# A transformer block's feed-forward: transposes of sixteen pieces, and transposes by quadrant with an exchange through HBM

## The reference

```python
h2 = rms_norm(x, norm_ffn_g[l])
u = jnp.square(jax.nn.relu(jnp.einsum('bsd,df->bsf', h2, w_up[l])))    # 2048 -> 8192
x = x + jnp.einsum('bsf,fd->bsd', u, w_down[l])                        # 8192 -> 2048
return rms_norm(x, norm_final_g)
```

## Time and profile before

| | us |
|---|---|
| median of 3 runs (1476.13 to 1476.44) | 1476.15 |
| the profiled execution | 1476.18 |
| its span, first to last instruction | 1474.4 |
| TensorE busy | 1465.7 |
| VectorE busy | 1190.9 |
| ScalarE busy | 766.8 |
| 16 transposes of one block (VectorE) | 7.0 |

### The profile page before, as it was taken

The page is one execution under the profiler, slowest core; times in us unless marked ns, Lnnn a source line. Parts: engine busy times, 40 slices in busy tenths (PEclk is TensorE's granted clock), DMA queues, the critical chain, the costliest instruction groups (busy, mean ns, idle before and its releaser), DMA issues.

```text
span 1474.4 us, 18772 instructions
## 1 busy us (share of the span) xinstructions
PE 1465.7 (99%) x6968; PEld 1279.8 (87%) x6968; DVE 1190.9 (81%) x1558; ACT 766.8 (52%) x986; POOL 15.0 (1%) x21
## 2 busy tenths in 40 slices
PE   9999999999999999999999999999999999999997
PEld 8888888888888888888888888888888888888886
DVE  7977887776577788777799988888897888889877
ACT  7656565444455555444445555555554555555553
POOL 0000000000000000000000000000000000000000
PEclk9999999999999999999999999999999999999999
DMA  9556544667655566556765665656666656655563
GB/s 333 191 169 211 184 154 164 229 203 241 213 180 184 186 199 206 194 200 200 248 233 181 202 219 201 218 185 207 217 204 202 208 199 226 214 199 193 198 209 114
DMA packets 149801, 299.33 MB, mean 203 GB/s; under 512 B 5232, under 2 KB 5360, under 8 KB 149488
## 3 DMA queue, kind: packets, MB, share of 16 engines
q1 hardware_dynamic: 149168, 297.51, 59.9%
q10 hardware_dynamic: 576, 1.06, 0.2%
HBM read 296.45 MB, written 2.10 MB: 202 GB/s over the span
## 4 chain that ended last, share of the span: by engine, by line
PE 98%; issue 1%; DVE 1%; POOLq 0%; POOL 0%; DVEq 0%; ACT 0%
PE acc L545 88%; PE acc L827 3%; PE banks L776 3%; PE acc L776 1%; PE banks L564 1%; PE banks L583 1%; PE banks L573 0%; PE banks L591 0%; DVE ta_lo L1775 0%; PE banks L680 0%; PE banks L696 0%; PE banks L695 0%; PE banks L693 0%; PE acc L603 0%; DVE final L1787 0%
## 5 line engine op out<-in xcount | busy, mean ns | idle before, releaser
L865 ACT ACTIVATE whi<-raw 128x1024 fp32r<-128x1024 f32 x542 | 569.2, 1056 | 577.3 <-PE acc L545 517.9
L1222 DVE TENSOR_TENSOR wlo<-raw,whi 128x1024 fp32r<-128x1024 f32 x542 | 655.1, 1223 | 213.1 <-ACT whi L865 208.5
L545 PE MATMUL acc<-whi,ta_hi 128*128 128x512 f32 x1308 | 497.4, 380 | 0.0
L545 PE MATMUL acc<-wlo,ta_hi 128*128 128x512 f32 x1308 | 495.7, 379 | 0.0
L545 PE MATMUL acc<-whi,ta_lo 128*128 128x512 f32 x1308 | 495.7, 379 | 0.0
L545 PEld LDWEIGHTS acc<-whi,ta_hi 128*128 128x128 f32 x1308 | 247.2, 189 | 36.7 <-issue 1.2
L545 PEld LDWEIGHTS acc<-whi,ta_lo 128*128 128x128 f32 x1308 | 247.2, 189 | 35.1
L545 PEld LDWEIGHTS acc<-wlo,ta_hi 128*128 128x128 f32 x1308 | 247.3, 189 | 34.5
L545 PE MATMUL acc<-whi,tb_hi 128*128 128x512 f32 x560 | 212.3, 379 | 0.0
L545 PE MATMUL acc<-wlo,tb_hi 128*128 128x512 f32 x560 | 212.2, 379 | 0.0
L545 PE MATMUL acc<-whi,tb_lo 128*128 128x512 f32 x560 | 212.2, 379 | 0.0
(11 more groups left out here) (208 smaller groups left out, 1049.2 us busy)
## 6 DMA issues: line engine op xcount, KB each, us to landing
raw<-in_w_in SPq DMA_DIRECT2D x64, 1024.0 KB, 5.2
raw<-in_w_up SPq DMA_DIRECT2D x64, 1024.0 KB, 5.3
raw<-in_w_down SPq DMA_DIRECT2D x57, 1024.0 KB, 5.0
raw<-in_w_gate SPq DMA_DIRECT2D x32, 1024.0 KB, 5.3
raw<-in_w_att SPq DMA_DIRECT2D x16, 1024.0 KB, 5.0
raw<-in_w_ret SPq DMA_DIRECT2D x16, 1024.0 KB, 5.0
raw<-in_w_out SPq DMA_DIRECT2D x16, 1024.0 KB, 5.0
raw<-in_w_down SPq DMA_DIRECT2D x14, 512.0 KB, 4.3
```

The costliest lines, as they stand in the source:

```text
L545: last = nc.tensor.matmul(paired(acc[B.parity][:, t, :]), a[:, k, tok], halves_in_turn(b), start=(k == 0 and n == 0), stop=(k == (B.ends + ...
L865: nc.scalar.activation(whi[:, B.ring_at(u), :], raw[:, B.raw_at(u), :], ACT.Copy).then_inc(hi_ready, 1)
L1222: V_.tensor_tensor(wlo[:, at, :], raw[:, B.raw_at(u), :], whi[:, at, :].bitcast(f32), ALU.subtract).then_inc(lo_ready, 1)
```

## The change

The feed-forward's turns are done in two steps. `turn_in_quads` (VectorE) does four transposes of 128x256; each transposes 32x32 blocks inside its own quadrant of 32 partitions, and reads every fourth column, so that what is left to do is an exchange between quadrants. ScalarE issues the exchange: `park` stores the 512 KB block into a scratch tensor in HBM, `fetch` loads it back into `buf[1]` with the quadrants exchanged, in runs of 256 floats (1 KB). The fetch waits for the store to have landed (`parked`) on ScalarE. The splits into `tb_hi` and `tb_lo` read `buf[1]` in runs of 32. The four transposed pieces lie in `buf[3]`.

With that, the order and the waits around the turns are rewritten. A new class `Quarter` gives the blocks; its parameters lead to the same groups in the same places. The weight sums lie elsewhere: T2 in `buf[3]`. The load of the last norm's gain (`gfin`) moves from stage 4 to the end of SyncE's queue. In the last quarter the last two units of D0 and D1 are worked after the first six of both.

```diff
+            def park(n, g):
+                act.wait_ge(quads_turned, n)
+                act.dma_start(parking[g], in_quads.rearrange("p o n -> p (o n)")).then_inc(parked, 16)
+            def fetch(g, n):
+                act.dma_start(exchanged_at.rearrange("p i a n -> p i (a n)"),
+                              parking[g].rearrange("(i f) (o n) -> (f o) i n", f=SQ, o=QUADS)).then_inc(exchanged, 16)
+            def fetch_next(Q, q, i, first):
+                act.wait_ge(parked, (q * 4 + i) * 16)
+                if i > 1:
+                    act.wait_ge(t_free, q * 4 + (T_STAGE6 + i - 1))
...
+                fetch(i - 1, Q.turn(q, i))
@@ ScalarE, an up block
+                    split(E, 0, 2)
+                    if i > 1:
+                        hi_from_exchanged(Q.turn(q, i - 1), i - 2)
+                    split(E, 2, 4)
...
+                        squared_relu(Q.up[i - 1][1])
...
+                        split(E, 4, 6)
+                        if i:
+                            park(q * 4 + i, i - 1)
+                        split(E, 6, 7)
+                    if i:
+                        fetch_next(Q, q, i, first)
+                    split(tail, 7, 8)
@@ ScalarE, from D1 on
+                split(Q.down[1], 0, 1)
+                park(q * 4 + 4, 3)
+                split(Q.down[1], 1, 3)
+                fetch_next(Q, q, 4, first)
...
+                split(Q.J, 0, 2)
+                if not last:
+                    hi_from_exchanged(Q.turn(q, 4), 3)
+                mixed_hi_of(GROUPS - 1, q * MIXES_OF_QUARTER)
                 if last:
+                    residual_squares(Q.down_end[0], 0, down_sq, buf[1])
+                if Q.boundary:
+                    split_for_seven(Q.boundary, Q.J, 2, Q.down_end[1] if last else None)
@@ ScalarE, split_for_seven
-                sums_hi(G, 0)
-                sums_hi(G, 1)
-                split(B, 5, 6)
-                sums_hi(G, 2)
-                split(B, 6, 9)
+                sums_hi(G, 0, 1)
+                sums_hi(G, 1, 3)
+                sums_hi(G, 2, 3)
+                split(B, u - 1, u + 3)
@@ VectorE, before
-                split(B[5], 3, 4)
-                mixed_tokens(q)
-                split(B[5], 4, 6)
-                dve.wait_ge(mixed_hi_ready, q + 1)
-                V_.tensor_tensor(mixed_lo[:], mixed, mixed_hi[:].bitcast(f32), ALU.subtract).then_inc(mixed_lo_ready, 1)
...
-                split(B[6], 0, 3)
-                add_residual(B[5], 1)
-                split_for_seven(G, B[6])
@@ VectorE, after
+                if last:
+                    split(Q.down[1], 0, 4)
+                    lo_from_exchanged(q * 4 + 16, 3)
+                    split(Q.down[1], 4, 6)
+                    split(Q.down_end[0], 6, 8)
+                    split(Q.down_end[1], 6, 7)
+                    add_residual(Q.down_end[0], 0)
+                    split(Q.down_end[1], 7, 8)
...
+                split(Q.J, 0, 1)
+                split(Q.J, 1, 2)
+                mixed_tokens(Q.turn(q, 4), q * MIXES_OF_QUARTER)
+                if not last:
+                    lo_from_exchanged(q * 4 + 16, 3)
...
+                split(Q.J, 2, ready)
+                mixed_lo_of(GROUPS - 1, q * MIXES_OF_QUARTER)
+                add_residual(Q.down_end[1], 1)
...
+                    split(Q.J, ready, G.at - 2)
+                    sums_for_seven(G, q * 4 + 4, G.mixed)
+            def turn_in_quads(n):
+                dve.wait_ge(u_ready, n)
...
+                strided = buf[0][:].rearrange("p t (m f o) -> p m t f o", o=QUADS, f=SQ)
+                for o in range(QUADS):
+                    piece = V_.transpose(in_quads[:, o, :].rearrange("p (m t n) -> p m t n", t=TILES, n=SQ), strided[:, :, :, :, o])
+            def sums_for_seven(G, parks, mixes):
...
+                V_.tensor_tensor(T1, left_up, right_up, ALU.add).then_inc(sum_set, 1)
+                dve.wait_ge(raw_full[E.slot(u + 2)], E.filled(u + 2))
+                dve.wait_ge(mixed_lo_ready, mixes)
+                V_.tensor_tensor(T3, right_up, right_low, ALU.add).then_inc(sum_set, 1)
+                split(E, u - 2, u - 1)
...
+                V_.tensor_tensor(T2, T1, right_low, ALU.add).then_inc(sum_set, 1)
                 sums_lo(G, 0)
+                split(E, u - 1, u)
+                dve.wait_ge(sum_set, G.sums(3))
+                V_.tensor_tensor(right_up, T2, left_low, ALU.add).then_inc(sum_set, 1)
                 sums_lo(G, 1)
+                split(E, u, u + 2)
                 sums_lo(G, 2)
```

More of the change, by code:

```diff
@@ L490, in load_right, with load_up @@
                 sp.dma_start(raw[:, E.raw_at(u + 1), :], parts[1]).then_inc(corner_full, 16)
-            def stage6(q, first, last=False):
-                B = quarter(q, first, last)
-                if first:
-                    load_block(B[0], w_up, q * D)
-                else:
[L497 to L509, removed]
+            def load_up(Q, q, i):
+                (E, tail), G = Q.up[i], Q.late[i]
+                col = q * D + i * COLS
+                load_rows(E, w_up, col, 0, range(3))
+                if G:
+                    load_left(G, q * D - D)
+                    load_right(G, q * D - D)
+                load_rows(tail, w_up, col, 0, range(3, 4))
@@ L761, in stage6 @@
-                gemm(B[5], tb_hi, tb_lo, 0, B[5].ends + 1)
-                gemm(B[6], tb_hi, tb_lo, 0, UNITS - 2)
-                if not last:
+                Q = Quarter(q, first, last)
+                for i in range(GROUPS):
+                    (E, tail), G = Q.up[i], Q.late[i]
+                    if first and i == 0:
+                        pe.wait_ge(h2T_ready, 3)
+                        gemm(E, ta_hi, ta_lo, 0, 6)
+                        pe.wait_ge(first_half, T_STAGE5 + 4)
+                        gemm(E, ta_hi, ta_lo, 6, 7)
+                        pe.wait_ge(h2T_ready, 4)
+                        gemm(E, ta_hi, ta_lo, 7, 8)
+                    else:
+                        gemm(E, ta_hi, ta_lo, 0, 6)
+                        if G:
+                            seven_products(G)
+                        gemm(tail, ta_hi, ta_lo, 6, 8)
@@ L832, in rest @@
             def rest(B):
-                for u in range(2, UNITS):
+                for u in range(B.ends + 1):
                     pe.wait_ge(lo_ready, B.low(u))
@@ new lines, in stage6 @@
+                split(Q.down[0], 0, 2)
+                hi_from_exchanged(Q.turn(q, 3), 2)
+                split(Q.down[0], 2, 4)
+                act.wait_ge(quads_turned, q * 4 + 3)
+                if Q.late[3]:
+                    act.wait_ge(sum_lo_ready, Q.late[3].halves(3))
+                squared_relu(Q.up[3][1])
+                if Q.units[0] > 4:
+                    split(Q.down[0], 4, 6)
+                split(Q.down[1], 0, 1)
+                park(q * 4 + 4, 3)
+                split(Q.down[1], 1, 3)
```

427 lines of the change are left out of this document (266 added, 161 removed).

## The result

The changed kernel takes 1498.37 us (median of 4 runs, 1498.08 to 1498.68) against 1476.3 for the kernel before on the same chip: a ratio of 1.0149, 95% interval 1.0132 to 1.0167. It is slower by 1.5%. The prediction was 1498.6. The profiled execution took 1498.08, its span is 1496.3, 21.9 more than before.

The account below looks back on a forecast made before the run. The prediction took TensorE (98% of the chain) as the bound. Lost cover in the boundary groups (11.5), the last quarter's (7.4) and late groups (3.5) added 22.4 to 1476.2: 1498.6 us, 8-in-10 range 1485 to 1514.

Parts of the forecast that it names:

- The sum, 22.4: Total predicted loss in us: boundary groups 11.5, last quarter's boundary group 7.4, late groups 3.5.
- Turns, 1.7 us each, hidden: VectorE's four 128x256 transposes per block: 1.7 us, or 7.0 if quadrants run serially; TensorE gains nothing.
- the walk: The prediction's instruction-by-instruction tracing of starts, waits and ends through up blocks and groups, using durations from the old profile.
- Exchange, 4.5 us each way, hidden: Each block's 512 KB store and load through HBM: about 4.5 us each, ends 3.4 and 8.2, no TensorE loss.
- the rival: Late exchange: transfers near 8.2 us each way lose 0.8 us in 12 of 16 turns, 1508 us; chance 0.09.
- the rule of the Trainium skill on strided copies: Rival: a fetch 19 times slower, 65 us, some 60 us late in 16 blocks, near 2400 us; chance 0.01.
- Boundary groups, 3.85 each: In quarters 1 to 3, the second product of the boundary group comes 3.85 us late, 11.5 us in all.
- the late mixed tokens: Boundary groups: mixed tokens now made behind J.1's split, so the first sum T1 starts 2.92 us late.
- the inner order: New order of sums and splits inside seven-product groups, lengthening T1 to second product; 0.93 us per boundary group.
- Last quarter, 7.4: Last quarter's boundary group: D0's residual add waits for D0's end and the second product comes 7.4 us late.
- Late groups, 3.5: Late groups of quarters 2 to 4: T1 stays, the order behind it costs 1.0, 1.0 and 1.55 us.
- Not slower, because VectorE has run ahead: Rival: lighter VectorE keeps the cover, J.5's lo starting by 1262.0 instead of 1265.9; 1476 us; chance 0.10.

Follow-up runs that it names:

- e4: Changed kernel with all orders put back (mixed tokens, last quarter, inside the groups); four-quadrant turns and exchange stay: 1476.60 us, ratio 1.0000 to the kernel before.
- e5: e4 with each turn's four transposes run, waited for and run again: 1488.95 us, ratio 1.0083 to the kernel before.
- e6: e4 with each transpose reading 256 elements in a row instead of every fourth, so values are wrong: 1476.46 us, measured once.
- e1: Changed kernel with only the old order inside the seven-product groups restored, mixed tokens still late: 1488.04 us, ratio 1.0079 to the kernel before.
- e12: Kernel before the change, with only the mixed tokens and their halves moved late, behind J.1: 1484.16 us, ratio 1.0049 to the kernel before.
- e2: Changed kernel with mixed tokens back ahead of block J in quarters 1 to 3 only: 1490.38 us, ratio 1.0095 to the kernel before.
- e3: e2 plus the last quarter: mixed tokens behind D1's fourth split, D0's residual add behind J.0: 1483.69 us, ratio 1.0051 to the kernel before.
- e9: Changed kernel with D0's residual add moved behind J.0's split in the last quarter only: 1495.83 us, ratio 1.0132 to the kernel before.
- e10: e9 plus D0's squares on ScalarE moved ahead of the mixed tokens' upper half: 1494.83 us, ratio 1.0122 to the kernel before.
- e8: e4 with one more seven-product late group in each of quarters two to four, in the third up block: 1492.78 us, ratio 1.0111.
- e7: e4 with every exchange store and fetch done twice, waiters waiting for both: 1478.10 us, ratio 1.0011 to the kernel before.

## Why the prediction was right, step by step

- **TensorE is the bound, and its matmuls don't change.** Shown: 6968 in both, and the seven groups hold 21.6 of the 21.9 us.
- **The sum, 22.4.** The medians differ by 22.1. That the forecast came within 0.3 us is partly chance: its terms are 0.8 too large in all, and the medians differ by 0.5 more than the table's sum.
- **Turns, 1.7 us each, hidden.** Hidden was right (e4, e5). The size was wrong: 3.1 us, between the ends 1.7 and 7.0. I weighed partitions and not the stride; e6 shows the reverse. The cover that I gave it stands: the walk had 1.4 us lost with a turn of 7.0, and e5's turn of 6.2 loses 0.7. The rule in the Trainium skill, Vector Engine (DVE) Microarchitecture Reference, section 3.8, was right on the quadrants, by e6's 413 ns; but it says nothing of a stride, and read as it stands it would have the strided transposes near 436 too; they are 833.
- **Exchange, 4.5 us each way, hidden.** Sum right by luck (9.0 for 9.0), parts off: the store lands in 2.8, below the lower end of 3.4, the fetch in 6.2. Hidden: e4. With both doubled, 11.7 us for the two, the twelve turns that the rival named lose nothing, as the walk has it (its price was for 16.4, which no run has); the 1.7 us are lost at a fourth turn. The prediction called that one hidden at both ends; in the last quarter its cover is the thinnest. That the rule of the Trainium skill on strided copies (VectorE: DVE Perf Modes, section The three transpose paths: 19 times slower) does not apply here is shown by the 6.2.
- **Boundary groups, 3.85 each.** Total right (3.73 to 3.77), split wrong. I booked 2.92 for the late mixed tokens and 0.93 for the inner order (the order inside the group). Alone, the first costs 1.8 to 2.0 (e1, e12), the second 0.8 to 1.1 (e2, e3). The reason stands in the rows of before: 0.64 us of idle time ahead of the fold and 0.4 of cover (it was done that long before TensorE needed it), 1.04 of slack. From T1 to the second product e1 needs 14.48 us with a full queue (1262.30 to 1276.78), the changed kernel 16.33 (1267.30 to 1283.63). So the inner order adds 1.85, not 0.93, and 1.88 is VectorE's wait for J.5's upper half; the 15.56 of before, against which I took the difference, held the slack (15.56 - 14.48 = 1.08). The mixed tokens' 2.92 were 2.85 by the trace: T1 starts 10.40 after J.1's upper half, before 7.55. Then 2.92 - 1.04 = 1.88 alone, 1.85 - 1.04 = 0.81 alone, and together 2.92 + 1.85 - 1.04 = 3.73. The walk came out right because it followed each instruction to the end and so spent the slack once.
- **Last quarter, 7.4.** Measured 7.23, and its parts: residual 2.2, squares 1.2 (by e9 and e10), the rest 3.8.
- **Late groups, 3.5.** Measured 3.1. The walk's 16.49 us from T1 to the second product were 16.33 in the third quarter's boundary group and 16.43 in quarter 4's late group.
- **Not slower, because VectorE has run ahead (0.10).** Refuted: VectorE was 61.5 us lighter, and stood idle for ScalarE and TensorE at the places that mattered. J.5's lower half, the sign that I named, started 18.0 us after J.1's upper half, where the walk had 18.2 and this rival 14.3.

Left open: how e8's groups would fare with buffers of their own for T1 and T2, which was not tried, and why the granted clock fell in the changed kernel's last group.

## What to carry to other kernels

When one engine is at 98% and stays so, price a change by the deadlines that its order moves, not by the work that it saves. Where two delays share one slack, neither has a price of its own: walk them together, and subtract the idle time that the old rows show once. A difference of two durations from a trace is the cost of the order only if neither contains slack, time in which the chain waited for something outside it.

## What the runs showed of the hardware

- A 128x256 float32 transpose on VectorE that reads every fourth element takes 833 ns, one that reads in a row 413, no more than one on 32 partitions (436).
- A 512 KB store to HBM landed in 2.8 us, the fetch back, which moves whole 1 KB runs to other partitions, in 6.2. A second such transfer on the same queue, issued 0.4 us behind the first, added 1.8 and 1.0 us until both had landed (e7): most of the 6.2 is not the data's time. The Trainium skill, in DMA: Bandwidth & Descriptors, section Anatomy of one DMA, gives about 2.0 us plus the bytes at 436 GB/s for DMAs that GpSimd issues, 3.2 us for 512 KB (an estimate by that formula). Here ScalarE issues them; the store is near that, the fetch nearly twice it.
